# The last two slabs of w_out and of the down projections, one token tile after the other

## The reference

```
o = concat(o_mla, o_gla) @ w_out
x = x + gate_m * rms_norm(o, g_post_mix)              # block 1, mixer
h = rms_norm(x, g_pre_ffn) * (1 + scale_f) + shift_f
f = (silu(h @ w_ffn_gate) * (h @ w_ffn_up)) @ w_ffn_down
x = x + gate_f * rms_norm(f, g_post_ffn)              # block 1, FFN
...                                                   # block 2, mixer
f = (silu(causal_dwconv(h @ w_gate)) * (h @ w_up)) @ w_down
h = h + rmsnorm(f, g_post_ffn)                        # block 2, FFN: the output
```

## Time and profile before

| | us |
|---|---|
| median of 3 runs (2526.32 to 2532.3) | 2530.67 |
| the profiled execution | 2528.7 |
| its span | 2526.9 |
| PE busy | 2342.8 (93%) |
| PEld busy | 2180.1 (86%) |
| DVE busy | 1544.0 (61%) |
| ACT busy | 1095.3 (43%) |
| POOL busy | 129.6 (5%) |
| mean granted TensorE clock | 0.958 of full speed |

### The profile page before, as it was taken

One profiled execution on the slowest core, in us unless ns is written; L12 is line 12 of the kernel. 1 busy time (PEld: TensorE's weight loads), 2 busy tenths in 40 slices (PEclk: granted clock), 3 DMA queues, 4 the chain that ended last, 5 costly groups with the idle time before them and its releaser, 6 DMA issues.

```text
span 2526.9 us, 41868 instructions
## 1 busy us (share of the span) xinstructions
PE 2342.8 (93%) x16346; PEld 2180.1 (86%) x16346; DVE 1544.0 (61%) x1728; ACT 1095.3 (43%) x1268; POOL 129.6 (5%) x248
## 2 busy tenths in 40 slices
PE   3989859799999999999799999997999999999996
PEld 3989747699998899998699996697999988999985
DVE  7958778845554467644554995545655644556545
ACT  4444363544444334433444435345444433344333
POOL 0000012100001100001200000000000011000011
PEclk9999979899999999999899998698999999999998
DMA  9978548655555577755365551153555555555542
GB/s 396 421 288 345 205 162 328 242 185 190 189 184 184 198 250 275 274 199 176 125 187 181 166 180 53 43 181 111 176 187 178 181 185 190 184 183 174 187 179 92
DMA packets 162948, 506.32 MB, mean 200 GB/s; under 512 B 8110, under 2 KB 12494, under 8 KB 134046
## 3 DMA queue, kind: packets, MB, share of 16 engines
q1 hardware_dynamic: 161536, 500.28, 56.5%
q0 software_dynamic: 752, 3.47, 0.5%
q10 hardware_dynamic: 576, 1.44, 0.2%
HBM read 503.06 MB, written 2.10 MB: 200 GB/s over the span
## 4 chain that ended last, share of the span: by engine, by line
PE 83%; DVE 6%; DMA 5%; ACT 4%; issue 2%; SPq 0%; ACTq 0%; DVEq 0%
PE pb L548 22%; PE pb L534 18%; PE pb L536 18%; PE pb L535 18%; DMA raw<-w_in 3%; DMA raw<-w_in_second 1%; DVE x L1523 1%; PE pb L646 1%; DVE wlo L435 1%; DMA raw<-w_ada 1%; DVE wlo L476 1%; PE pb L1022 0%; ACT whi L423 0%; PE pb L513 0%; PE pb L514 0%
## 5 line engine op out<-in xcount | busy, mean ns | idle before, releaser
L435 DVE TENSOR_TENSOR wlo<-raw,whi 128x1024 fp32r<-128x1024 f32 (+1 forms) x716 | 866.2, 1219 | 795.8 <-ACT whi L423 795.4
L423 ACT ACTIVATE whi<-raw 128x1024 fp32r<-128x1024 f32 (+1 forms) x716 | 749.0, 1054 | 1105.4 <-PE pb L536 718.0
L534 PE MATMUL pb<-xh,whi 128*128 128x256 f32 (+2 forms) x3760 | 1066.8, 284 | 8.7 <-DVE accf L1586 3.2
L535 PE MATMUL pb<-xl,whi 128*128 128x256 f32 (+2 forms) x3760 | 1066.5, 284 | 0.0
L536 PE MATMUL pb<-xh,wlo 128*128 128x256 f32 (+2 forms) x3760 | 1065.8, 283 | 0.0
L534 PEld LDWEIGHTS pb<-xh,whi 128*128 128x128 f32 x3760 | 712.8, 190 | 10.5 <-issue 4.0
L535 PEld LDWEIGHTS pb<-xl,whi 128*128 128x128 f32 x3760 | 713.9, 190 | 0.0
L536 PEld LDWEIGHTS pb<-xh,wlo 128*128 128x128 f32 x3760 | 712.6, 190 | 0.0
L548 PE MATMUL pb<-whi,stg 128*128 128x512 f32 x1664 | 449.9, 392 | 15.6 <-DVE xl L1500 7.5
L548 PEld LDWEIGHTS pb<-whi,stg 128*128 128x128 f32 x1664 | 314.2, 189 | 83.7 <-DVE xl L1500 8.2
L548 PE MATMUL pb<-wlo,stg 128*128 128x512 f32 x832 | 258.8, 392 | 0.0
(11 more groups left out here) (371 smaller groups left out, 1780.8 us busy)
## 6 DMA issues: line engine op xcount, KB each, us to landing
raw<-w_ada SPq DMA_DIRECT2D x79, 1024.0 KB, 6.6
raw<-w_ffn_gate SPq DMA_DIRECT2D x44, 1024.0 KB, 5.2
raw<-w_ffn_up SPq DMA_DIRECT2D x44, 1024.0 KB, 5.2
raw<-w_ffn_down SPq DMA_DIRECT2D x44, 1024.0 KB, 4.8
raw<-w_gate SPq DMA_DIRECT2D x44, 1024.0 KB, 5.2
raw<-w_up SPq DMA_DIRECT2D x44, 1024.0 KB, 5.1
raw<-w_down SPq DMA_DIRECT2D x44, 1024.0 KB, 4.8
raw<-w_in SPq DMA_DIRECT2D x40, 1024.0 KB, 5.1
```

The lines of the kernel that those rows point to most:

```text
L423: act.activation(to, src, ACT.Copy).then_inc(hi_ready, 1)
L435: dve.tensor_tensor(to, src, hi, ALU.subtract).then_inc(raw_done, 1)
L534: mm(o, whi[:, s, t], xh[:, k, c0:c1], start=(k == 0), stop=False)
L535: mm(o, whi[:, s, t], xl[:, k, c0:c1], start=False, stop=False)
```

## The change

For w_out and for each of the four down projections, PE's last two slabs are taken together (`last_slabs`). For token tile 0 the four weight halves of both slabs are multiplied, then PE counts a new semaphore `rows_done`, then the same four halves for tile 1. The number of matmuls is the same. `used` is now counted by 2 behind each slab's part of tile 1. DVE takes the four banks of tile 0 at `rows_done`, and tile 1 at the end. Behind an FFN DVE also does tile 1's gain, and POOL does none; a few counts and waits follow from that, and two waits at the start of the kernel are joined in one. PE's second group waits for the two copies of tile 0 only.

```diff
+    def last_slabs(u, w, stg_n):
+        for t in range(NT):
+            for j in range(2):
+                if t == 0:
+                    pe.wait_ge(staged, stg_n + 2 * j)
+                for hh in range(2):
+                    if t == 0:
+                        pe.wait_ge(raw_done, 2 * (u + LAST_STEP[u >= U_FFN] * j) + hh + 1)
+                    last = products(w + 2 * j, j, t, hh)
+                if t:
+                    last.then_inc(used, 2)
+            if t == 0:
+                last.then_inc(sem("rows_done"), 1)
...
-    POST_AT = {4: 0, 5: 2, 6: 3, 7: 5}
+    POST_AT = {4: 0, 5: 2, 6: 4, 7: 6}
...
-                pe.wait_ge(sem("part_done"), 4 * (2 * b + g) - 1)
+                pe.wait_ge(sem("part_done"), 4 * (2 * b + g) - 2)
...
-            with pe.Fori(1, n) as i:
+            with pe.Fori(1, n - 1) as i:
                 for j in range(4):
                     slab(u + j, w + 2 * j, st + 2 * (j + 1), j % 2, False, i, 4, 8)
+            m = 4 * (n - 1)
+            for j in (m, m + 1):
+                slab(u + j, w + 2 * j, st + 2 * (j + 1), j % 2, False)
+            last_slabs(u + m + 2, w + 2 * m + 4, st + 2 * (m + 3))
...
+            def parts(t, ready):
+                dve.wait_ge(*ready)
+                for hh in range(2):
...
+            parts(0, (sem("rows_done"), 2 + 2 * b + g))
+            if g + 1 < len(GROUPS):
+                first_lo(u, w, hs=(0, 1))
+            else:
+                gained(0)
+            parts(1, (used, w))
...
-        pool.wait_ge(sem("gate_ready"), 1)
-        pool.wait_ge(sem("part_done"), 8)
-        pool.tensor_tensor(xs[:, 1, :], accf[:, 1, :], gateF[:, :], ALU.mult).then_inc(sem("o_gained"), 1)
...
+        act_row_stats(4, [(0, pb[:, 0:4, :])], lambda t: (sem("o_taken"), POST_AT[4] + 1))
         first_hi(U_FFN, W_FFN, hs=(0, 1))
-        act_row_stats(4, [(t, pb[:, 4 * t:4 * t + 4, :]) for t in (1, 0)],
-                      lambda t: (used, W_FFN) if t else (sem("o_taken"), POST_AT[4] + 1))
+        act_row_stats(4, [(1, pb[:, 4:8, :])], lambda t: (sem("o_taken"), POST_AT[4] + 2))
         first_hi(U_FFN, W_FFN, hs=(2, 3))
...
+        def post_ffn(n):
+            for t in range(NT):
+                if t:
+                    gained(n, t)
+                dve_post(n, t, xs[:, t, :], x[:, t, :], (sem("o_taken"), POST_AT[n] + t + 1), t + 1)
```

More of the change, by code:

```diff
@@ L118 @@
 AHEAD = 4
+LAST_STEP = (2, 1)
 BEHIND_ROW = (2, 2, 1, 2, 2, 1, 2, 2, 1, 2, 2, 1, 2, 2, 0, 0)
@@ L539, in chunk, with products @@
                 behind[1]()
-    def slab(u, w, stg_n, s, first, i=0, nu=0, nk=0, freed=None):
[L544 to L551, removed]
+    def products(w, s, t, hh, first=False):
+        ws = (w + hh) % SLOTS
+        for part, wt in ((0, whi), (0, wlo), (1, whi)):
+            for c in range(2):
+                last = mm(pb[:, 4 * t + 2 * hh + c, :], stg[:, s, part, t * P:(t + 1) * P],
+                          wt[:, ws, c * CW:(c + 1) * CW], start=first and part == 0 and wt is whi,
+                          stop=part == 1, skip_group_check=True)
+        return last
+    def slab(u, w, stg_n, s, first, i=0, nu=0, nk=0, freed=None):
         def split(hh):
@@ L563, in slab @@
                         split(hh)
-                    last = products(t, hh)
+                    last = products(w, s, t, hh, first)
             last.then_inc(used, 2)
@@ L1249, in act_ffn, with act_post_ffn @@
                 then()
-    def act_post_ffn(n):
-        act_row_stats(n, [(t, accf[:, t, :]) for t in range(NT)],
-                      lambda t: (sem("part_done"), 8 * (n // 2 - 1)))
+    def act_post_ffn(n, t):
+        act_row_stats(n, [(t, accf[:, t, :])], lambda t: (sem("part_done"), 8 * (n // 2 - 1) - 2 + 2 * t))
     def act_forget():
@@ L1524, in dve_post, with dve_ffn @@
         dve.wait_ge(sem(f"post{n}"), done)
-    def dve_ffn(b, u, w):
+    def dve_ffn(b, u, w, gained):
         c = CHUNK0 + sum(GROUPS) * b
@@ L1926, in _ @@
             slab(U_WOUT + 2 * j, W_WOUT + 2 * j, 2 * (j + 1), j % 2, j == 0)
-        with pe.Fori(1, KT // 4) as i:
+        with pe.Fori(1, KT // 4 - 1) as i:
             for j in range(4):
                 slab(U_WOUT + 2 * j, W_WOUT + 2 * j, 2 * (j + 1), j % 2, False, i, 8, 8)
+        for j in (12, 13):
+            slab(U_WOUT + 2 * j, W_WOUT + 2 * j, 2 * (j + 1), j % 2, False)
+        last_slabs(U_WOUT + 28, W_WOUT + 28, 30)
         pe.wait_ge(sem("o_taken"), POST_AT[4] + NT)
@@ L2179, in _ @@
             mod_sum(U_WOUT + 2 * k + 1, mods[:, 3, k:k + 1], b_col(3, k), col("g_pre_ffn", k))
-        dve.wait_ge(used, W_FFN)
         for t in range(NT):
-            if t:
-                dve.wait_ge(sem("rms"), RMS_AT[4] + 1)
+            dve.wait_ge(*((used, W_FFN) if t else (sem("rows_done"), 1)))
             dve_gained(4, pb[:, 4 * t:4 * t + 4, :], by_bank(adaA[:, :]), by_bank(xs[:, t, :]))
@@ L2246, in _ @@
         dve_split_x(NQ, sem("turned_out"), 3 * KT)
-        dve_ffn(1, U_FFN2, W_FFN2)
-        dve.wait_ge(sem("g3_in"), 16)
-        dve.wait_ge(sem("part_done"), 16)
-        dve_gained(7, accf[:, 0, :], gateF[:, :], xs[:, 0, :])
-        for t in range(NT):
-            dve_post(7, t, xs[:, t, :], x[:, t, :], (sem("o_gained"), 3) if t else (sem("o_taken"), POST_AT[7] + 1), t + 1)
+        dve_ffn(1, U_FFN2, W_FFN2, lambda t: gained(7, t))
+        post_ffn(7)
     stack.close()
```

41 lines of the change are left out of this document (16 added, 25 removed).

## The result

| | before | after |
|---|---|---|
| median of the runs | 2531.49 (2526.32 to 2534.63, 4 runs) | 2511.41 (2510.67 to 2512.3, 4 runs) |
| profiled execution, its span | 2528.7, 2526.9 | 2511.81, 2510.0 |
| mean granted clock of it | 0.958 | 0.964 |

The changed kernel is faster: ratio 0.9923, 95% interval 0.9906 to 0.9940. Two further measurements, on other chips, gave 0.9916 and 0.9924.

A forecast was written before the change was run, and what follows sets the result against it. PE, busy 93% of the span, was taken as the bound, so only its stalls and the end count. 1.35 + 3.2 + 3.9 + 4.3 = 12.75 us gave 2515.9, or 2517.9 from the median; forecast 2517.0, range 2512 to 2523.5.

The forecast's parts named there:

- the second addition: Sign behind block 1's FFN: it comes 9.9 us after PE's end instead of 13.8.
- the scaling behind w_out: Sign: DVE's scaling of tile 1 comes 12.2 us after PE's end instead of 13.6.
- the last store's wait: Sign at the kernel's end: it ends 15.2 us after the last matmul instead of 19.5.
- One sign of being wrong: In a tile 0 pass, PE's L548 waits for `wlo` or for the staging.
- A: Rival, TensorE clock: earlier starts behind w_out and block 1's FFN meet half clock, 2 to 3 us each; 2521.9; chance 0.12.
- B: Rival, supply: PE starves in w_out's tile 0 pass and at the seams, or POOL blocks; about 2522; chance 0.10.
- C: Rival: late `gate_ready` holds DVE's early gain and tile 1's sums; 2537 if the load takes 20 us longer; chance 0.03.
- D: Rival: ACT's squares of tile 1 or splits late behind the FFNs, new order worth half; 2521; chance 0.05.
- the end of block 1's FFN: Term: tile 0's sums and gain run early, without POOL's product beside DVE; 3.9 us gained.
- The end of the kernel: Term: last addition ends 7.5 us after the sums instead of 11.78, last store 5.3 us behind; 4.3 us gained.
- w_out: Term: tile 0's gain starts early, row tile 1's scaling at 486.7 instead of 488.06; 1.35 us gained.
- The seams: Term: PE's 1.59 us wait for the third copy between each FFN's groups becomes 0; 3.2 us together.

The follow-up runs named there:

- e6: Changed kernel with two extra unused 2.3 us DVE products between the additions behind block 1's FFN; 2518.90 us.
- e15: Changed kernel with group 0 of each FFN in the old order (seams as before), measured again; 2517.78 us.
- e7: Changed kernel with ACT's second pair of splits behind w_out moved behind the sums of the new x; 2510.88 us.
- e3: Changed kernel, but POOL multiplies tile 1 by its gain behind both FFNs, as before; 2522.82 us, ratio 0.9960.
- e11: Changed kernel, but tile 0's final store waits for tile 1's addition, so both stores are issued together; 2516.17 us.
- e12: Kernel before with both tiles' gains behind the FFNs on DVE, none on POOL, old slab order; 2527.70 us, ratio 0.9984.
- e8: Changed kernel with the seam between the groups of each FFN as before; 2518.63 us.
- e2: Changed kernel with w_out's last slabs and the work behind them in the old order; 2510.68 us.
- e14: Changed kernel with w_out's last slabs and what follows in the old order, measured again; 2511.59 us.
- e5: Changed kernel with one extra unused 2.3 us DVE product between the additions behind block 1's FFN; 2517.68 us.
- e16: Changed kernel with PE filler transposes of constants, 96 behind block 1's FFN and 84 behind w_out; 2513.21 us.
- e13: The changed kernel measured again, unaltered; 2512.43 us, ratio 0.9924 against the kernel before.

## Why the prediction was wrong

**The mechanism held, with one gap.** At the seams PE goes on without a wait, no DVE operation is above 2.4 us at either end, and the second addition comes 9.6 us instead of 9.9 behind block 1's FFN. Two of the intervals named there were shorter than forecast (the scaling behind w_out at 11.2 us for 12.2, the last store's wait at 13.9 for 15.2). One sign of being wrong did come: PE's weight load waited for the staging in w_out's tile 0 pass.
- A came in neither first chunk in the three profiles of the changed kernel, but inside the chunk behind w_out in e6 and e15, at 1.5 us each.
- B came in small at w_out: 0.3 us in the first profile, up to 1.4 in e7. At the seams no product waits. POOL blocked nothing: its memset (467.62 to 469.43) ran beside DVE's gain, which kept its 2.29 us.
- C did not come: `gate_ready` was 1 us early. In its price, 20 us later would have been some 2535 and not 2537, because 1.6 of the 20 us were slack.
- D did not come: ACT's root for tile 1 was in time at both ends.

**Mis-sized terms, 4.1 us in the trace.** The step that failed is the sum. It was too small at four places and 0.2 us too large at the end of block 1's FFN:
- The end of the kernel, 5.6 for 4.3. "The last store follows 5.3 us behind as before" is the part that failed: the change moved the first store out of the last one's way, and that gave 1.05 (e3 and e11 show the dependence, with e12 against it); the additions gave 0.2 more.
- The start of the last down projection, 1.6, not in the sum at all. Rival A looked for clock lost at first chunks; I had not asked where the kernel before loses clock behind short pauses. It is shown by e8 and e15 that the seams' old order brings it.
- w_out, 2.0 for 1.35. I put DVE's last sum at its old place, 4.6 us before PE's end; it ended 6.4 us before it, so `rows_done` and not the sum set the start, 0.8 us sooner. The old place was one execution's: in the other five profiles with the old order it is 5.3 to 5.9. The scaling came 2.4 us sooner, and the late staging took 0.3 back.
- The seams, 3.7 for 3.2. The 1.59 us of the row is the wait alone; between the same matmuls each seam cost 1.8 to 1.9.

**The range.** From the profiled execution the sum gave 2515.9, the four terms make 2511.8, and the profiled run was 2511.81. (That this fits to 0.1 is luck: the untouched stretches, +0.9 and -0.6, and the 0.2 of block 1's FFN nearly cancel.) I had then set 1.1 us on top, for the median above that execution. That was the wrong way: executions of the kernel before lie above its profile because of its clock (0.954 to 0.960 in 52 executions), and the changed kernel has 0.960 to 0.965 in 13. The three runs that I had spread over 6 us, and that spread should have been read as clock that a shorter wait might give back. The two kernels' mean clocks can't be set against each other as they stand, though: half clock granted while PE has nothing to do counts in them, and behind PE's last matmul that is 16.3 us before and 10.6 after.

**What stays open.** w_out's part is 2 us at its place and nothing measurable in the whole (e2, e14). Why the seams' order moves a stretch of half clock isn't known, nor why e12's last store was late. The medians of e3, e5, e6 and e11 lie 1 to 4 us above their traces' account.

## What to carry to other kernels

Where a last stage feeds a chain of row-wise work, finish one tile's rows first: the early half of the chain goes under the matmuls, and the first store leaves early. Then check every input of the reordered pass: not only the weights but the staged activations are needed sooner. Don't let a GpSimd product of two SBUF operands run beside a VectorE operation with two SBUF operands on the critical chain (6.69 us for 2.35 in e3). When sizing a wait, compare starts of the same matmul on both sides, and look at the granted clock behind every pause, not only at those that the change touches.

## What the runs showed of the hardware that was not expected

- Keeping TensorE busy through a wait can cost time: with the filler its clock fell in the turns at 1252.5 instead of in the wait, and the 200th matmul came 3.9 us later than in e13 (one profile each, e16 and e13; the medians don't differ). The Trainium skill, on TensorE: Matmul & The Clock Gate, section "HAM oscillation — how this bites in real kernels", has the burst behind a wait throttled. The trace agrees for the turns, which in e13 start at 0.50. But the chunk behind them has full clock when the fall came early in the wait, and pays when it came late.
- A stretch of half clock comes with the old order of slabs at a seam 234 us earlier (in six profiles of six, and in none of twelve with the new order).
- Executions of one kernel on one core differ by up to 8 us, and follow the mean granted clock: 1.6 us for 0.001 of it by the medians at 0.956 and 0.959, 1.3 by a line through all 52.
- The span ends 4.3, 5.3 and 6.8 us behind the last addition with the two 1 MB stores 4.8, 2.6 and 0.4 us apart; e12, with 5.5 at 4.8 us, is the exception.
